# Loading one weight chunk of each expert in three transfers of 112, 8 and 8 rows

## What is computed

```python
probs = jax.nn.softmax(t @ w_router, axis=-1)
aff, idx = lax.top_k(probs.T, cap)                 # 64 and 32 tokens per expert
xe = t[idx]
hid = silu(einsum("ecd,edf->ecf", xe, w_gate)) * einsum("ecd,edf->ecf", xe, w_up)   # f = 2816
ye = einsum("ecf,efd->ecd", hid, w_down) * aff[..., None]
out = zeros_like(t).at[idx.reshape(-1)].add(ye.reshape(-1, d))
```

## Time and profile before

| | us |
|---|---|
| median of 3 runs (lowest, highest) | 2447.57 (2447.28, 2447.87) |
| profiled execution, span | 2445.6 |
| PE busy in the span | 2395.3 (98%) |
| first matmul of the experts (L2435) | 1044.3 |
| last matmul of L2435 starts | 2415.3 |

### The profile page before, as it was taken

One profiled execution on the slowest core, in us unless ns is written; L12 is line 12 of the kernel. 1 busy time (PEld: TensorE's weight loads), 2 busy tenths in 40 slices (PEclk: granted clock), 3 DMA queues, 4 the chain that ended last, 5 costly groups with the idle time before them and its releaser, 6 DMA issues.

```text
span 2445.6 us, 49821 instructions
## 1 busy us (share of the span) xinstructions
PE 2395.3 (98%) x22095; PEld 1636.4 (67%) x22095; DVE 1074.5 (44%) x2029; ACT 514.2 (21%) x1059; POOL 305.4 (12%) x418
## 2 busy tenths in 40 slices
PE   9899999999999999999999999999999999999996
PEld 9798999899898888845655544455455455455453
DVE  6989889888987634421121221112112121211213
ACT  5445444444534412100000000000000000000001
POOL 0313332441341000000000000000000000000001
PEclk9899999999999999999999999999999999999998
DMA  5133333223335536399999999999999999999996
GB/s 183 56 125 98 98 106 125 89 95 126 110 117 209 205 138 230 118 400 413 410 412 416 415 411 420 415 411 415 416 418 409 419 415 408 421 407 416 420 409 238
DMA packets 88486, 707.00 MB, mean 289 GB/s; under 512 B 11632, under 2 KB 15856, under 8 KB 51408
## 3 DMA queue, kind: packets, MB, share of 16 engines
q1 hardware_dynamic: 65360, 628.93, 63.4%
q0 software_dynamic: 14272, 56.60, 7.4%
q10 hardware_dynamic: 8640, 18.29, 2.0%
HBM read 669.72 MB, written 34.06 MB: 288 GB/s over the span
## 4 chain that ended last, share of the span: by engine, by line
PE 79%; DMA 17%; DVE 3%; issue 1%; ACT 1%; POOL 0%; ACTq 0%; POOLq 0%; DVEq 0%
PE p_gu L2435 28%; PE pp L1131 17%; DMA raw<-in_w_e 14%; PE p_y L2453 8%; PE pp L1339 6%; PE pp L1175 5%; PE p_y L2456 3%; PE pp L1368 2%; PE p_z L2456 2%; PE pdg L1226 2%; DMA raw_first<-in_w_e 2%; PE off_banks L1209 1%; PE ptr L1193 1%; PE pp L1447 1%; PE off_banks L1223 1%
## 5 line engine op out<-in xcount | busy, mean ns | idle before, releaser
L2435 PE MATMUL p_gu<-raw,xT 128*32 128x512 f32 (+1 forms) x8304 | 863.0, 558 | 11.7 <-DMA raw<-in_w_e 10.9
L2435 PEld LDWEIGHTS p_gu<-raw,xT 128*32 128x32 f32 x8304 | 366.9, 110 | 418.4 <-issue 321.9
L2331 DVE SCALAR_TENSOR_TENSOR tg<-tg,p_gu 128x256 f32<-128x256 f32 (+1 forms) x144 | 57.4, 399 | 1084.5 <-ACT tg L2295 1080.1
L2453 PE MATMUL p_y<-raw,hidT 128*32 128x384 f32 x3744 | 432.2, 486 | 0.0
L2295 ACT ACTIVATE tg<-p_gu 128x256 f32<-128x256 f32 (+1 forms) x144 | 52.7, 366 | 1283.5 <-PE p_gu L2435 1283.5
L2456 PE MATMUL p_y<-raw,hidT 128*32 128x256 f32 x1248 | 320.2, 379 | 0.0
L1131 PE MATMUL pp<-h_hi,wx_hi 128*128 128x256 f32 (+1 forms) x832 | 295.1, 355 | 0.5 <-ACT fo L717 0.5
L1131 PE MATMUL pp<-h_hi,wx_lo 128*128 128x256 f32 (+1 forms) x832 | 281.5, 338 | 0.0
L1131 PE MATMUL pp<-h_lo,wx_hi 128*128 128x256 f32 (+1 forms) x832 | 280.9, 338 | 0.0
L2453 PEld LDWEIGHTS p_y<-raw,hidT 128*32 128x32 f32 x3744 | 153.9, 110 | 87.9 <-issue 56.6
L2456 PE MATMUL p_z<-raw,hidT 128*32 128x256 f32 x624 | 185.6, 379 | 0.0
(11 more groups left out here) (283 smaller groups left out, 3315.0 us busy)
## 6 DMA issues: line engine op xcount, KB each, us to landing
raw<-in_w_e SPq DMA_DIRECT2D x185, 2048.0 KB, 38.1
raw<-in_w_e SPq DMA_DIRECT2D x58, 1536.0 KB, 35.6
raw_first<-in_w_e SPq DMA_DIRECT2D x23, 2048.0 KB, 39.0
w_raw<-in_w_x SPq DMA_DIRECT2D x48, 512.0 KB, 3.5
dec<-acs POOLq DMA_DIRECT2D x48, 512.0 KB, 4.8
raw<-in_w_e SPq DMA_DIRECT2D x16, 1024.0 KB, 38.0
w_raw<-in_w_g SPq DMA_DIRECT2D x24, 512.0 KB, 3.5
g_tab<-gx POOLq DMA_DIRECT2D x8, 1152.0 KB, 5.9
```

The source lines that it names most:

```text
L2331: dve.scalar_tensor_tensor(out=tg[:, r % 2, 0:w], in0=tg[:, r % 2, 0:w], scalar=1.0, in1=p[:, 0:w], op0=ALU.add, op1=ALU.mult).then_inc(s_ ...
L2435: mm = pe.matmul(p_gu[g][quad(q), 0:w], xT[:, e % 2, k * SLOTS + 32 * g:k * SLOTS + 32 * (g + 1)], slot[:, at:at + w], start=(k == 0), sto ...
L2453: pe.matmul(y_first[half][quad(g), :], hidden(g), w[:, half * 3 * P:(half + 1) * 3 * P], start=first, stop=last)
```

## The change

A chunk's transfer may be cut by rows. `row_parts(c)` gives the cuts: for the last gate/up chunk (i = KS - 1) of an expert's second block (b % NB == 1), one chunk of 18, they are rows 0 to 111, 112 to 119 and 120 to 127; for every other chunk they are all 128 rows. `load_part` issues one DMA for each cut, all to the same slot and semaphore, 16 for each. `landed(c)` counts what the slot's semaphore then has to show, and PE waits for that value instead. No byte more or less is loaded, and the order of the chunks stays.

```diff
+def row_parts(c):
+
+    kind, b, i = chunk(c)
+    if kind == "gu" and i == KS - 1 and b % NB == 1:
+        return (0, 112), (112, 120), (120, P)
+    return ((0, P),)
+
+
+def landed(c):
+
+    return 16 * sum(len(row_parts(before)) for before in range(c % RAW, c + 1, RAW))
+
+
 def load_part(sp, A, raw, s_raw, c):
...
     src = A["w_e"][e:e + 1, at * P:(at + w) * P].rearrange("e (p n) -> p (e n)", p=P)
-    sp.dma_start(raw[c % RAW][:, 0:w], src).then_inc(s_raw[c % RAW], 16)
+    for lo, hi in row_parts(c):
+        sp.dma_start(raw[c % RAW][lo:hi, 0:w], src[lo:hi, :]).then_inc(s_raw[c % RAW], 16)
...
             def loaded(kind, b, i):
 
                 c = CHUNK_OF[kind, b, i]
-                pe.wait_ge(s_raw[c % RAW], 16 * (c // RAW + 1))
+                pe.wait_ge(s_raw[c % RAW], landed(c))
                 return raw[c % RAW]
```

## The result

The changed kernel takes **2648.61 us** (2645.07 to 2669.08) where the kernel before takes 2447.33 us beside it: a ratio of **1.0834** (95% interval 1.0816 to 1.0852), 201 us slower, 12.6 us for each of the 16 splits. The forecast was 2440.9 us, the range 2437 to 2458; both are missed, on the side of rival (b) and by ten times its price. The profiled execution is one of the six runs, that of 2650.63 us.

The account below looks back on a forecast made before the run. The prediction took late weight transfers to set the pitch in the later part, with PE also nearly full. The row shift gained 6.7 us, issues, small packets and PE's wait cost 0: 2447.6 - 6.7 = 2440.9 us, range 2437 to 2458.

Parts of the forecast that it names:

- rival (b): The two short transfers of neighbouring rows collide in neighbouring partitions: 20.2 us lost, 2461.1 us, slower; chance 0.14.
- What bounds the kernel: In the later part weights, not PE, set the pitch; faster loading could give 33.4 us, slower loading costs without end.
- The rows: Cutting 112 + 8 + 8 rows moves 0.62 us an expert from one half of the engines to the other, gaining 6.7 us.
- laden eight: Eight engines that get 9 rows of the split chunk instead of 8; taken to be mostly the early ones.
- rival (a): Fetches are spread evenly or the laden half is already late: 0.62 us an expert later, 2457.5 us, slower; chance 0.15.
- gain of 6.7 us: Forecast saving from the row shift: 0.42 us an expert over 16 experts, between 5.3 and 8.2 us.
- The term g: Difference between early and late halves of the DMA engines, put at 1.04 us an expert from instruction fetches.
- The rule of the Trainium skill: Bandwidth goes by SBUF ports reached; the short transfers reach two each: about 3.6 us an expert, 58 us, some 2500 us.
- The issues: 32 more transfers issued on SP at 0.328 us, 10.5 us, covered by SP's waits for slots: cost 0.
- the small packets: Two more transfers bring one more packet under 512 B each per engine used: taken as 0, at most 0.40 us an expert.
- PE's wait: PE waits for a higher value of the same semaphore: no cost.
- Rival (c): Nothing moves: each engine keeps its load, or small packets eat the gain; 2447.6 us, chance 0.19.

Follow-up runs that it names:

- the run with extra rows: Kernel before, no split, plus two 8-row transfers (8 KB rows, steps of four in rows 0 to 29) behind each expert's smallest chunk: 2457.50 us, ratio 1.0041.

## Why the prediction was wrong, point by point

**What bounds the kernel** held. The stream of weights sets the pitch and its loss is paid in full: by the last expert the stream is 200.0 us late and the kernel 201 us. The note that slower loading has no such end as faster loading was the part to take seriously.

**The rows** is the step that failed, in two places. First, "112 rows are 7 for each of 16 engines" was taken as costless beyond its bytes. In the changed kernel the stream runs at 262 and then 208 GB/s while the 112 rows of the first split are under way, and the cut into 112 and 16 rows, without a short transfer, costs more than the change. Second, the premise that the laden eight are the early half: two of them are late, as far as sorted landing times tell. Extra rows on them cost 9.6 us, which is rival (a) at its price of 9.9. Even without any collision, there was no gain of 6.7 us to be had. The reading from which the premise came was of the order in which sixteenths begin and end; it was right for six of eight, and a maximum over engines forgives none. The size of the shift, 0.62 us a row, was right: a row of 16 KB takes 0.61 us. The term g was put at 1.04 us an expert from the instruction fetches; in the kernel before the first and last sixteenth come apart by 1.4 to 1.7 us an expert (3.4 us at expert 0, 25.0 and 24.6 at experts 13 and 15), and no run shows what makes them. The 32898 rows of queue q1 left out that some of the short packets are the indirect queue's; they are 33346, of 15.0 KB, which changes nothing behind it.

**Rival (b)** named the right kind of mechanism, a collision in the partitions, and its sign, stretches well under 400 GB/s, is what the profile shows. But it looked at the short transfers alone, and at how closely their rows lie. Its price, 16 x 1.26 = 20.2 us, came from an indirect transfer and allowed only for the two short ones. Measured by themselves in half the bytes, those cost 31.7 us, 9.6 of it the load. The transfer of 112 rows was not in it at all. The price was also taken as the same for every split; the first costs 7.5 us, and one where the engines are 20 to 26 us apart 16 to 19 us.

**The rule of the Trainium skill** on ports (page "SBUF — State Buffer", section "Door 1: The DMA port swizzle") spoke against the change and I gave it a small chance, with an estimate of 2500 us for the two short transfers alone. The traces agree with it for the cut at row 64 (210 and 206 GB/s) and for the even and odd rows (409 and 421). Counting ports is not enough, though. By the same page rows 0 to 111 reach all sixteen ports, and eight rows in steps of four reach eight in either half. Here the 112 rows went at 208 to 262 GB/s, and such eight rows cost 9.6 us in one half and 30.8 us in the other.

**The issues, the small packets and PE's wait** were each put at 0. Three transfers cut by columns put all of them to the proof: 2.6 us at the medians. The issue itself stays at 0.328 us (median) in the changed kernel; cut by columns it is 0.431 us. Held, to within 5 us.

**Rival (c)**, that nothing moves, is out: the landing times of the run with extra rows show that eight engines and not sixteen take a short transfer.

**The range** was as wide as the bounds of the rivals made it; the end that reached to (b) was cut off for having a low chance, and that end itself was the term mis-sized by ten.

## What to carry to other kernels

By these runs, a load that fills all DMA engines should keep all 128 partitions in every transfer; if it has to be cut, cut it by columns, or by rows in steps that run over all 128 partitions (even and odd). Rows in steps within one half are no remedy: in 64 to 93 they cost as much as packed ones. Before a shift of load between engines is costed, ask which of them the end waits for: here two late ones among eight turned the sign. And a disturbance of a shared stream meets every engine at its own time, so its price can grow with the distance between the first and the last of them: here from 7 to 18 us, up to some 25 us of distance.

## What the runs showed of the hardware

Two transfers of 64 rows run at 210 and 206 GB/s cut into neighbouring rows, 1.24 us for a row of 16 KB, and at 409 to 421 GB/s cut into even and odd ones, 0.61 us a row. Two extra transfers of eight rows cost three times as much in partitions 64 to 93 as in 0 to 29. Cuts by rows of quite different shape (112 + 16, 120 + 8, 64 + 64, 112 + 8 + 8) all end within 2649 to 2668 us. After a wait of PE for weights the granted clock of the stretch from 2162 to 2168 us is 0.72 in the changed kernel:

```profile
2162.00:2168.00 6.00, 4.48 (x36) 2.49 (x36) 0.00 (x0) 0.00 (x0) 0.00 (x0) 0.72 1.04 363
2168.00:2178.00 10.00, 8.67 (x75) 3.22 (x79) 0.00 (x0) 0.00 (x0) 0.00 (x0) 0.83 1.00 428
```

That is a mean of the two levels: 0.50 (1.2 GHz) from 2163.7 to 2166.9 us, behind 2.8 us in which PE stood still, and 1.00 (2.4 GHz) around it. Over the span the granted clock is 0.965 instead of 0.993. An estimate from these two is 0.028 x 2648 = 74 us for a PE that never waits, so the clock can make up the 60.3 us by which PE is busier. How much of these lies on the path is open: the late weights would have held PE up anyway, and no run took the one without the other.
